# Stick and mLSTM gates and projections: operand halves side by side in 512-column products, summed on VectorE

## The reference

```python
gates = jax.nn.sigmoid(gate_pre + b_gate[l]).reshape(bsz, seq, N_BRANCH, D_MODEL)
mixed = (gates[:, :, 0] * (y_sb @ w_sb_proj[l])
         + gates[:, :, 1] * (y_ml @ w_ml_proj[l])
         + gates[:, :, 2] * (y_x @ w_x_proj[l]))
x = x + mixed @ w_out[l]
u = _rmsnorm(x, g_mlp[l]) @ w_ff1[l]
x = x + jnp.square(jax.nn.relu(u)) @ w_ff2[l]
```

## Time and profile before

| | before |
|---|---|
| median of 3 runs | 1230.73 us |
| profiled execution, its own time | 1229.82 us |
| span of its trace | 1228.0 us |
| mean granted clock of TensorE | 0.994 |
| TensorE busy | 1209.6 us, 99% |
| VectorE busy | 815.0 us, 66% |
| ScalarE busy | 672.2 us, 55% |
| chain that ended last | TensorE 90%, VectorE 5%, ScalarE 4% |
| stick stage, mLSTM stage | about 347 to 393 us, 393 to 439 us |

### The profile page before, as it was taken

How to read it: one execution, slowest core, us unless ns; L and a number is a source line. 1 busy time by engine, 2 the same in 40 slices (tenths; PEclk the granted TensorE clock), 3 DMA queues, 4 the chain that set the end, 5 groups by cost and what they waited for, 6 DMA issues and landing times.

```text
span 1228.0 us, 22431 instructions
## 1 busy us (share of the span) xinstructions
PE 1209.6 (99%) x9840; PEld 1189.8 (97%) x9840; DVE 815.0 (66%) x914; ACT 672.2 (55%) x806; POOL 11.0 (1%) x24
## 2 busy tenths in 40 slices
PE   9999999999999999999999999999999997999997
PEld 8999999999999999999999999999999997999997
DVE  7866676777655566775547748888874555777443
ACT  7543545676543445454344559898964444555332
POOL 0000000000000000000000000000000000000000
PEclk9999999999999999999999999999999998999999
DMA  9543545455655545556565646565456553555750
GB/s 328 171 149 104 159 151 146 147 159 168 198 180 175 187 155 171 173 191 220 174 193 177 189 129 198 155 196 165 147 189 196 184 167 113 172 172 177 234 173 35
DMA packets 210689, 210.80 MB, mean 172 GB/s; under 512 B 6540, under 2 KB 207628, under 8 KB 210592
## 3 DMA queue, kind: packets, MB, share of 16 engines
q1 hardware_dynamic: 207904, 200.30, 51.5%
q0 software_dynamic: 2112, 8.17, 2.2%
q10 hardware_dynamic: 576, 0.90, 0.2%
HBM read 208.25 MB, written 1.09 MB: 170 GB/s over the span
## 4 chain that ended last, share of the span: by engine, by line
PE 90%; DVE 5%; ACT 4%; DMA 1%; issue 1%; DVEq 0%; ACTq 0%
PE ps L241 81%; PE ps L1570 6%; DVE w_lo L209 2%; PE ps L1619 1%; ACT w_hi L203 1%; PE ps L1573 1%; DVE arena L1173 1%; PE ps L250 1%; DMA arena<-rows 0%; DMA pcol<-in_params 0%; ACT L629 0%; DVE arena L1202 0%; ACT L437 0%; ACT x_hi L454 0%; DVE res L1318 0%
## 5 line engine op out<-in xcount | busy, mean ns | idle before, releaser
L241 PE MATMUL ps<-x_hi,w_hi 128*128 128x256 f32 x2480 | 712.8, 287 | 6.6 <-DVE x_lo L1282 6.1
L241 PE MATMUL ps<-x_hi,w_lo 128*128 128x256 f32 x2480 | 702.6, 283 | 0.0
L241 PE MATMUL ps<-x_lo,w_hi 128*128 128x256 f32 x2480 | 702.6, 283 | 0.0
L209 DVE TENSOR_TENSOR w_lo<-raw,w_hi 128x2048 fp32r<-128x2048 f32 x187 | 427.6, 2291 | 225.6 <-ACT w_hi L203 225.6
L241 PEld LDWEIGHTS ps<-x_hi,w_hi 128*128 128x128 f32 x2480 | 476.6, 192 | 12.0 <-issue 8.8
L241 PEld LDWEIGHTS ps<-x_lo,w_hi 128*128 128x128 f32 x2480 | 476.8, 192 | 0.8
L241 PEld LDWEIGHTS ps<-x_hi,w_lo 128*128 128x128 f32 x2480 | 476.6, 192 | 0.0
L203 ACT CAST w_hi<-raw 128x2048 fp32r<-128x2048 f32 x187 | 354.1, 1899 | 108.2 <-PE ps L241 107.4
L241 PE MATMUL ps<-w_hi,x_hi 128*128 128x256 f32 x480 | 136.7, 285 | 0.0
L241 PE MATMUL ps<-w_lo,x_hi 128*128 128x256 f32 x480 | 135.8, 283 | 0.0
L241 PE MATMUL ps<-w_hi,x_lo 128*128 128x256 f32 x480 | 135.7, 283 | 0.0
(11 more groups left out here) (216 smaller groups left out, 765.8 us busy)
## 6 DMA issues: line engine op xcount, KB each, us to landing
raw<-in_w_in SPq DMA_DIRECT2D x170, 512.0 KB, 4.7
raw<-in_w_ff SPq DMA_DIRECT2D x64, 512.0 KB, 4.5
raw<-in_w_up SPq DMA_DIRECT2D x32, 512.0 KB, 4.7
raw<-in_w_down SPq DMA_DIRECT2D x32, 512.0 KB, 4.4
raw<-in_w_mem_kv SPq DMA_DIRECT2D x16, 512.0 KB, 6.0
raw<-in_w_out SPq DMA_DIRECT2D x16, 512.0 KB, 5.0
raw<-in_w_ssm_proj SPq DMA_DIRECT2D x16, 512.0 KB, 4.6
raw<-in_w_x_proj SPq DMA_DIRECT2D x8, 512.0 KB, 4.6
```

What stands on the lines that cost most here:

```text
L209: nc.vector.tensor_tensor(w_lo[:, s], raw[:, s], w_hi[:, s].bitcast(FP32), ALU.subtract)\
L241: last = nc.tensor.matmul(dst, l, r, start=start and k == 0 and m == 0, stop=stop and k == nk - 1 and m == 2)
```

## The change

The high and low parts of the activations move into one tensor `x_hl` [128, 40, 2, 256], so that the two parts of a tile lie side by side. For the stages "gs" and "gm", `pair_products` makes per k-step one product of 512 columns (w_hi x [x_hi, x_lo]) into a whole bank, and then, after all k-steps, one product of 256 columns each (w_lo x x_hi) into the bank's first half. A half of a unit now takes a whole bank, a unit two: gate units use banks 5 and 6, projection units banks 3 and 4. VectorE sums the two halves of each bank (a reduction over a strided view of 2 x 512 elements to 2 x 256) into `gt` for the gate and `gp` for the projection. The sigmoids of ScalarE follow in place on `gt`, after the sum. VectorE then multiplies gp by gt in SBUF and adds into `mix`.

VectorE's order in a pair becomes: split, sum of the gate, split, sum of the projection, product, addition (and the low part). TensorE waits, before a gate or projection unit, for the sum of the one before it in the same banks, and after the last pair for the eighth gate sum. The wait for the last mLSTM low part (`y_lo` 12) moves from before "gm" to before "gs".

```diff
@@ -30,7 +30,7 @@
         base[name] = len(filled)
-        filled += [not (name.startswith("down") or name == "gq" and k % 3) for k in range(n)]
+        filled += [not (name.startswith("down") or name in ("gs", "gm") or name == "gq" and k % 3) for k in range(n)]
     before = [sum(filled[v] for v in range(u % SLOTS, u, SLOTS)) for u in range(len(filled))]
@@ -114,8 +114,8 @@
         w_lo = sb("w_lo", [P, SLOTS, KT, CW], FP32R)
-        x_hi = sb("x_hi", [P, OPND, T], FP32R)
-        x_lo = sb("x_lo", [P, OPND, T], FP32R)
+        x_hl = sb("x_hl", [P, OPND, 2, T], FP32R)
+        x_hi, x_lo = (x_hl[:, :, n, :] for n in range(2))
         res = sb("res", [P, KT, T])
@@ -124,7 +124,7 @@
         tab = sb("tab", [P, TAB])
-        thin_hi, thin_lo = (v[:, 30:32, :].rearrange("p a b -> p (a b)")[:, 0:40 * KT] for v in (x_hi, x_lo))
+        thin_hi, thin_lo = (x_hl[:, n].rearrange("p a b -> p (a b)")[:, 0:40 * KT] for n in (30, 31))
         small = sb("small", [P, 640])
@@ -169,9 +169,9 @@
         x_row = cells(7168, T)
-        n_hi, n_lo = (v[:, M0:M0 + 3, :].rearrange("p a b -> p (a b)").rearrange("p (h c) -> p h c", h=2)
-                      for v in (x_hi, x_lo))
-        ones_r, later_r = (x_hi[:, M0 + 3, n * P:(n + 1) * P] for n in range(2))
+        n_hi, n_lo = (x_hl[:, n:n + 2].rearrange("p a b c -> p (a b c)")[:, 0:768].rearrange("p (h c) -> p h c", h=2)
+                      for n in (M0, M0 + 2))
+        ones_r, later_r = (x_hi[:, M0 + 4, n * P:(n + 1) * P] for n in range(2))
         dtc, acs = (small[:, n:n + 64].rearrange("p (t h) -> p t h", t=2) for n in (256, 320))
@@ -242,6 +242,28 @@
             return last
+        def pair_products(u, o, at, dst, start=True, stop=True, ks=range(KT)):
+            s, cols = u % SLOTS, slice(o * P, (o + 1) * P)
+            for k in ks:
+                nc.tensor.matmul(dst, w_hi[:, s, k, cols], x_hl[:, at + k], start=start and k == 0, stop=False)
+            for k in ks:
+                last = nc.tensor.matmul(dst[:, 0], w_lo[:, s, k, cols], x_hi[:, at + k], start=False,
+                                        stop=stop and k == KT - 1)
+            return last
+        def out_banks(b):
+            return ps[:, 3:5] if b % 2 == 0 else ps[:, 5:7]
+        def stick_banks(n):
+            return ps[:, 5:7] if n else ps[:, 0:2]
+        def gate_banks(n):
+            return ps[:, 3:5] if n else ps[:, 5:7]
         def thin_products(dst, c0, n, at):
@@ -266,6 +288,7 @@
         gt = cells(3344, 2, T)
+        gp = cells(0, 2, T)
         a_q, a_k, a_v, a_bias, a_p, a_pT = (cells(0, 2, T), cells(512, 2, T), cells(6144, 2, T), cells(1536, 4, 384),
@@ -548,7 +571,7 @@
                     evac(U("cross", i, 2, 3), s_v)
-                    A(x_hi[:, M0 + 3], cst[:, P:3 * P], ACT.Copy).then_inc(S("sums_r"), 1)
+                    A(x_hi[:, M0 + 4], cst[:, P:3 * P], ACT.Copy).then_inc(S("sums_r"), 1)
             for i in range(1, 5):
@@ -698,10 +721,20 @@
             gated("gx", 3, 16, 3)
+            def gated_pair(i, k, n):
+                split()
+                act.wait_ge(S("gate_sum"), n - 3)
+                for c in range(2):
+                    last = A(gt[:, c], gt[:, c], ACT.Sigmoid, bias=pc("b_gate", 2 * i + k + c))
+                last.then_inc(S("gate_open"), 1)
+                split()
             for i in range(4):
-                gated("gs", i, 0, 4 + i)
+                gated_pair(i, 0, 4 + i)
             for i in range(4):
-                gated("gm", i, 8, 8 + i)
+                gated_pair(i, 8, 8 + i)
                 mixed(i, 8 + i)
@@ -956,6 +989,11 @@
                 V.tensor_copy(dst, unit_bank(u)).then_inc(taken(u), 1)
+            def evac_pair(u, dst, banks):
+                finished(dve, u)
+                V.tensor_reduce(dst, banks.rearrange("p o (a t) -> p o t a", a=2), AXX, ALU.add).then_inc(taken(u), 1)
             def bc(v, n, at=1):
@@ -1270,10 +1308,31 @@
             gated("gx", 3, True)
+            def sum_pair(u, dst, n):
+                finished(dve, u)
+                return V.tensor_reduce(dst, gate_banks(n).rearrange("p o (a t) -> p o t a", a=2), AXX, ALU.add)
+            def gated_pair(stage, i, n, lo=None):
+                u, v, dst = U(stage, i, 0, 2), U(stage, i, 1, 2), rows(mix, 2 * i, 2)
+                split()
+                dve.wait_ge(S("p_used"), n + 1)
+                sum_pair(u, gt, 0).then_inc(S("gate_sum"), 1)
+                split()
+                sum_pair(v, gp, 1).then_inc(S("proj_sum"), 1)
+                dve.wait_ge(S("proj_sum"), n - 3)
+                dve.wait_ge(S("gate_open"), n - 3)
+                chain(tt(gp, gp, gt, ALU.mult))
+                tt(dst, dst, gp, ALU.add).then_inc(S("p_used"), 1)
+                if lo is not None:
+                    low(2 * i + M0, dst, "mix_hi", lo, "mix_lo")
             for i in range(4):
-                gated("gs", i, False)
+                gated_pair("gs", i, 4 + i)
             for i in range(4):
-                gated("gm", i, False, i + 1)
+                gated_pair("gm", i, 8 + i, i + 1)
             def lower(src, g, b, splits, at=H0, names=("n_hi", "n_lo")):
@@ -1585,6 +1644,14 @@
                     last.then_inc(S(f"unit{u % SLOTS}"), 1)
+            def pair_half(u, o, at, banks):
+                if o == 0:
+                    begin(u)
+                last = pair_products(u, o, at, banks[:, o].rearrange("p (a b) -> p a b", a=2))
+                if o == 1:
+                    last.then_inc(S(f"unit{u % SLOTS}"), 1)
             def unit(u, at, tok=FP, nk=KT, lo=None):
@@ -1821,11 +1888,22 @@
             pe.wait_ge(S("y_lo"), 8)
+            pe.wait_ge(S("y_lo"), 12)
+            def gated_pair(stage, i, at, n):
+                need(pe, "gate_sum", n)
+                for o in range(2):
+                    pair_half(U(stage, i, 0, 2), o, H0, gate_banks(0))
+                need(pe, "proj_sum", n)
+                for o in range(2):
+                    pair_half(U(stage, i, 1, 2), o, at, gate_banks(1))
             for i in range(4):
-                gated("gs", i, YSB)
-            pe.wait_ge(S("y_lo"), 12)
+                gated_pair("gs", i, YSB, i)
             for i in range(4):
-                gated("gm", i, YML)
+                gated_pair("gm", i, YML, 4 + i)
+            pe.wait_ge(S("gate_sum"), 8)
             def norm(n, b):
```

## The result

The changed kernel takes 1237.89 us (median of 5 runs, 1237.14 to 1239.44), the kernel before 1230.73 us (1230.31 to 1232.12): ratio 1.0058, 95% interval 1.0047 to 1.0070, 7.2 us slower. The profiled execution took 1237.86 us, its span is 1236.1 us (before 1229.82 and 1228.0).

A forecast was written before the change was run, and what follows sets the result against it. TensorE's work, or a new TensorE wait, was taken to bound the kernel. Profiled 1229.8 + 4.6 (waits less savings) + 1.1 (clock) = 1235.5 us; the median lay 0.9 higher, so 1236.4 us, range 1233.0 to 1242.5.

The forecast's parts named there:

- TensorE's side: Stick and mLSTM units: a k-step takes 0.347 us instead of 0.360, saving 3.4 us over 256 steps.
- The fixed part of 2.5 ns: Skill page's fixed time per TensorE product, by which the saving would be 0.6 us; the prediction held the rows against it.
- the 131 ns: Skill page's time for 512 columns with weight loads, by which the saving would be over 25 us; prediction rejected it.
- The sum: VectorE's new reduction of 1,024 elements to 512 per bank pair: 1.20 us, bounds 1.1 and 1.4 us.
- slow-sum rival: VectorE's strided sum takes 1.7 to 2.3 us, so the stick round does not fit either: 1243 to 1253 us, chance 0.13.
- The stick round: Stick stage: VectorE and ScalarE need 10.95 us a pair, TensorE 11.09; no TensorE wait, all 4 pairs gain.
- The mLSTM round: mLSTM stage: the cast waits behind x_hi's write, making first sums 13.53 us apart, 2.44 us over TensorE's 11.09.
- S of the fourth pair: Start of the first (gate) sum in the fourth mLSTM pair, forecast at 437.6 us.
- The waits: TensorE waits 0.6 and 0.6 us in the fourth mLSTM pair, 1.8 for the last gate sum, 4.7 in the first out unit.
- The low part of the last pair: x_lo of the last mLSTM pair, needed by the first out unit after 36 products, ready at 447.8 against 443.2 us.
- The 0.2 us at the first norm sum: After the out units: the norm's first pair is ready at 455.2, TensorE wants it at 455.1; 0.2 us more lost.
- The clock: TensorE's clock falls behind the new 4.7 us hole, likelier than not, costing 1.1 us; bounds 0 and twice that.

The follow-up runs named there:

- the run with the stick stage alone: Changed kernel with the mLSTM stage back on the old gate code, so only the stick stage is changed: 1229.16 us against 1230.01 for the kernel before.
- the run with the shorter copy: Changed kernel, but VectorE copies only each bank's first half (0.69 us) instead of summing both halves: 1233.37 us against 1230.13 for the kernel before.
- the run with spare products: Changed kernel plus 36 unread 256-column products in TensorE's wait for the mix's last low part: 1235.95 us against 1230.13 for the kernel before.
- the run with the mLSTM stage alone: Changed kernel with the stick stage back on the old gate code, so only the mLSTM stage is changed: 1238.26 us against 1230.01 for the kernel before.

## Why the prediction was right

The forecast was 1236.4 us, the median is 1237.9; direction, mechanism and place were as told. By its steps:

**TensorE's side.** 512 columns were taken at 0.227 us from the slope of the 384-column rows; they take 0.230. The rows allowed that number: the starts of 178.51 and 178.86 lie two products of 384 columns apart, 0.175 us each and not 0.173, and the slope from there leads to 0.230. With 0.119 us for those of 256 columns a unit takes 5.59 us, not 5.55. The gain is 16 x (5.76 - 5.59) = 2.7 us instead of 3.4. This is the term that was off most, by 0.7 us: small per product, but there are 256. Nine of the 16 units lie ahead of the first mLSTM sum, so a little over half of it, 0.4 us, reached the end; behind that sum VectorE's rounds set the pace. The fixed part of 2.5 ns and the 131 ns that the page "TensorE: Matmul & The Clock Gate" of the Trainium skill gives (section "Back-to-back issue gap") both stay refuted for this stream: 256 columns take 120 ns and 512 take 230.

**The sum.** Taken at 1.20 us, measured at 1.23. The inner stride of 256 elements and the 512 outputs cost nothing beside a plain reduction of 1,024 elements, so the slow-sum rival fell.

**The stick round.** Told as 10.95 us of VectorE and ScalarE against 11.09 us of TensorE; measured, it fits into 11.17 us with 0.17 us to spare, where 0.14 was told. The run with the stick stage alone shows that it gains.

**The mLSTM round.** 13.53 us told, 13.57 us measured. S of the fourth pair was put at 437.6 and is 438.21. The order as its cause is shown by the runs that change nothing but the order, and the part of the sum's duration in it by the run with the shorter copy: 1.1 us less per round, 2 x 0.54.

**The waits.** 0.6, 0.6, 1.8 and 4.7 us told; the trace puts 1.0 us (two waits), 1.5 us and 4.5 us on record. The low part of the last pair was to come at 447.8; it comes at 448.48. The 0.2 us at the first norm sum did not show, since the slower products ahead of it hid it; in the run with spare products, with the clock up, it is there (0.66 against 0.43 us).

**The clock.** Told as likelier than not and 1.1 us; it fell, and the run with spare products puts its price at 1.24 us. What the prediction did not say is how much this price varies: 2.3 us in the run with the mLSTM stage alone, 2.7 us behind the shorter hole of the copy run (both against the 7.46 us of the spare products, one execution each), none behind a wait of 1.8 us. Its bound, twice 1.1 us, was too small for two of these.

**The sum of it all.** In the profiled executions 6.5 us are lost up to the out stage, where 5.7 were told. The low part of the last pair came 0.7 us late against the forecast: 0.5 us because the first mLSTM sum starts at 397.48 and not at 397.0 (nine shortened units lie before it), 0.1 by the three rounds, 0.1 by the last pair's own path. The restart behind the wait was taken at 0.03 us and is 0.26 (the row of 12 products in 2.82 us already held 0.3 us more than 12 x 0.21); the clock cost 0.1 more, the first norm sum 0.2 less. Another 1.5 us of difference between the two traces lies in two later places. They are not caused by the change as far as the runs show: between the hole ahead of the second MLP and the long piece in that MLP there are 55.4 us before and 56.4 after, and in the four experiments without any new wait 55.3, 56.0, 56.1 and 56.2; at ScalarE's exponentials TensorE waited 1.1 us before, 1.6 after, and 1.2 to 1.6 in the eight experiments. The first of the two is the clock behind that hole, which comes back earlier in one trace than in the other, as the stretches above show. Why it does was not tried, nor was the cause of the second.

## What to carry to other kernels

Where two engines prepare the operands of a third, add up the round that their fixed orders make, hand-over by hand-over, and hold it against the third engine's pace; shares of 50 to 70% say nothing about it. When a step moves from a quick reader to one that must wait for another engine, look at what stands behind it in its queue: here a cast of weights that needed nothing of the sum, and exchanging two calls turned a loss of 7.2 us into a gain of 1.8 us. A lag that grows by 2.4 us a pair stays invisible for three pairs and is paid where the stage ends, so a fast engine that is late only at a seam points back to the rounds before it.

## What the runs showed of the hardware

A hole of 3.5 us in TensorE's work cost more clock (2.7 us) than one of 4.5 us (1.24 us in the full change, 2.3 us with the mLSTM stage alone), and one of 1.8 us cost none. Each is one profiled execution. Behind one and the same hole, the one ahead of the second MLP, the way to the long piece took 55.3 to 56.5 us in the ten traces. So the price of a hole is not told by its length, and it varies where nothing was changed. Filling it with products that nobody reads took the price away and cost nothing, since the operands were there.

A reduction by VectorE over a strided view of PSUM, two elements per output, ran at the pace of a plain one: 1.23 us for 1,024 elements, against 1.21 us for 1,024 elements in SBUF with 4 outputs.
